# HGRN projections as three passes of rounded operands, with the input split in its norm and the weights split by ScalarE and GpSimd

## The chip, the cores and the metric

The kernel runs on one core of a Trainium2 chip. The metric is the device time of one execution in microseconds.

## The reference, cut to what matters

The program runs three blocks one after another on 512 tokens of width 1024. The change touches the first half of the first block, an HGRN mixer with 16 heads of 128 columns. The part of it that the projections feed:

```python
h  = modulate(x,   norm_g[0], shift,   scale)      # 512 tokens
hc = modulate(ctx, norm_g[0], shift_c, scale_c)    # 256 context tokens
# hgrn_w_in: (1024, 5 * 2048), columns q | v | f forward | f backward | gate
q, v, zf, zb, g = split(h  @ hgrn_w_in)            # q and gate only for the 512 tokens
vc, zfc, zbc    = split(hc @ hgrn_w_in)            # v and both f also for the context
# f = lb + (1 - lb) * sigmoid(z), k = 1 - f; a gated linear recurrence over the tokens,
# forward and backward, started from the context; then an RMS norm per head,
# times silu(g), and a product with hgrn_w_out
```

All inputs and outputs are float32.

## The kernel before, in words

The program is a row of phases. Each phase is one block in which every engine has its own instruction stream, ordered against the others by semaphores that are counted up and waited for; the phases follow one another. `norm_phase` (L382) writes the normed and modulated input to `K.hT` (128 partitions x 8 k-tiles x 512 tokens) and in place to `K.ctxT` (8 x 256). Its ScalarE squares the tiles, TensorE sums them (L417), VectorE takes the reciprocal (L431) and scales each of 8 + 8 tiles (L434), and ScalarE adds the shift with an Identity (L408).

`hgrn_phase` (L438) then works head by head. For head h, TensorE's `project` (L525) makes eight groups of sums over 8 k-tiles, in the order V for the tokens, V for the context, ZF tokens, ZF context, ZB tokens, ZB context, Q, G, which take turns in four PSUM banks (`ps[n % 4]`). In the V groups the input is the stationary operand and the weights, 128 columns wide, are the moving one (L536); there are 4 + 2 tiles of tokens. In the others the weights are stationary and 512 or 256 tokens move (L540). All operands are float32, and the profile shows two records, a weight load and a matmul each, for every float32 product.

The order on TensorE is project(h), then recur(h-1) (L566): the transposes (L574, L576), the scores in small blocks (L550 to L562), the products with kT (L586, L588), the outputs (L592, L597) and a sum for the norm (L601). ScalarE evacuates the groups (L618): a copy for V, Sigmoid for ZF and ZB into `hg_sig`, Silu for Q and G. Between the evacuations it has the logarithms and exponentials of the head before (L632, L638), then the copies of kT (L655). VectorE prepares gates, scans and products (`prepare`, L705) and the states of the recurrence (`recur`, L751). The sigmoids, q and gate have two buffers each, by the parity of the head.

Each of the five weight pieces of a head (128 x 8 x 128, 512 KB) has a buffer of its own, `hg_w0` to `hg_w4`. SP refills it when the last group that reads it has been summed (L503 to L504), and TensorE waits for the transfer itself:

```python
if c == 0:
    pe.wait_ge(w_in[m], 16 * h + 16)
if n >= 4 or not first:
    pe.wait_ge(evac, NG * h + (n - 3))
```

GpSimd only makes masks at the start of this phase (L510 to L521). Other phases, all of `product_phase` (L785), already use three passes of rounded operands: ScalarE rounds the weights to float32r (L865), GpSimd subtracts the rounded from the full ones (L833), and TensorE adds high x high, low x high and high x low in PSUM (L849 to L851), with 512 moving columns in each. `ho`, `m`, `ff`, `mg`, `pb` are tags of such phases.

Of the kernel before, what the change touches and what calls it, by code (L numbers as in the profile page):

```python
# [5 lines left out]
F32 = mybir.dt.float32  # L6
F32R = mybir.dt.float32r
# [430 lines left out]
def hgrn_phase(K, hO):  # L438
# [3 lines left out]
    hT, cT = K.hT, K.ctxT  # L442
# [8 lines left out]
    with ExitStack() as st:  # L451
        W = [K.sb(st, f"hg_w{m}", [P, KD, P]) for m in range(5)]
        vt = [K.sb(st, f"hg_v{i}", [P, NT // P, P]) for i in range(2)]
        sg = [[K.sb(st, f"hg_sig{i}{d}", [P, NT]) for d in range(2)] for i in range(2)]
        qs = [K.sb(st, f"hg_q{i}", [P, T]) for i in range(2)]
        gs = [K.sb(st, f"hg_gate{i}", [P, T]) for i in range(2)]
        f1 = [K.sb(st, f"hg_f{d}", [P, NT]) for d in range(2)]
        kk = [K.sb(st, f"hg_k{d}", [P, NT]) for d in range(2)]
        cum = [K.sb(st, f"hg_cum{d}", [P, NT]) for d in range(2)]
        lev = [K.sb(st, f"hg_lev{d}", [P, 3, T]) for d in range(2)]  # L460
        dg = [K.sb(st, f"hg_diag{d}", [P, 2, T]) for d in range(2)]
# [9 lines left out]
        osq = K.sb(st, "hg_osq", [P, T])  # L471
# [8 lines left out]
        w_in = sems[0:5]  # L480
# [5 lines left out]
        LAST_OF = {V: 2, ZF: 4, ZB: 6, Q: 7, G: 8}  # L486
# [7 lines left out]
        with nc.Block() as block:  # L494
            @block.sync
            def _(sp):
                clear_old(sp, old)

                def load(h, first, shift=0):
                    at = h * P if first else sp.snap(h * P)  # L500
                    for m in (V, ZF, ZB, Q, G):
                        if not first:
                            sp.wait_ge(proj, NG * h + LAST_OF[m])  # L503
                        sp.dma_start(W[m][:, :, :], wv[:, :, bass.ds(at + (COL[m] + shift), P)]).then_inc(w_in[m], 16)  # L504
                load(0, True)
                with sp.Fori(0, NH - 1) as before:
                    load(before, False, P)
# [14 lines left out]

            @block.tensor
            def _(pe):
                def project(h, p, first=False):  # L525
                    for n, (m, c) in enumerate(GROUPS):
                        if c == 0:
# [3 lines left out]
                        src, w = (cT, TC) if c else (hT, T)  # L531
                        bank = ps[n % 4]
                        if m == V:
                            for t in range(w // P):
                                for k in range(KD):
# [30 lines left out]
                def recur(h, p, very_first=False):  # L566
# [34 lines left out]
                    pe.matmul(SC[:, :], K.ones[:, :], osq[:, :], start=True, stop=True).then_inc(ms_ok, 1)  # L601
# [12 lines left out]
            def _(act):  # L614
# [3 lines left out]
                def evacuate(h, p, groups):  # L618
                    for n in groups:
# [6 lines left out]
                        elif m in (ZF, ZB):  # L626
                            s = sg[p][m - ZF]
                            act.activation(ctx_cols(s) if c else lat_cols(s), bank[:, 0:TC if c else T], ACT.Sigmoid).then_inc(evac, 1)
                        else:
                            act.activation((qs if m == Q else gs)[p][:, :], bank[:, :], ACT.Silu).then_inc(evac, 1)  # L630
# [21 lines left out]
                def recur(h):  # L652
# [5 lines left out]
                    act.activation(osq[:, :], OUT[:, :], ACT.Square).then_inc(sq_ok, 1)  # L658
# [1889 lines left out]
```

## Time and profile before

| | us |
|---|---|
| median of 3 runs | 5039.47 (5036.48 to 5039.67) |
| the profiled execution, its time | 5038.89 |
| its span in the profile | 5037.1 |
| hgrn phase, first to last of its matmuls | 271.6 to about 1290 |
| one head in the steady loop | 61.96 |

The granted TensorE clock is 0.87 of full as a mean over the span. In the rows below, "PE" is TensorE's matmuls, "PEld" its weight loads, "DVE" VectorE, "ACT" ScalarE, "POOL" GpSimd. A matmul's duration covers its way through the pipeline, so its price in a stream is read from start to start. Where rows of a timeline say x16, sixteen records in a row are merged, and the time beside it runs from the first one's start to the last one's end.

### The profile page before, as it was taken

The numbers are of one execution on the slowest core, as the hardware profiler recorded it, in microseconds if no ns is written. First come the engines' busy times: TensorE is split into PE (matmuls) and PEld (weight loads), VectorE is DVE, ScalarE is ACT, GpSimd is POOL, SyncE is SP. The second block draws the span as 40 slices with busy tenths as digits, with TensorE's granted clock in tenths as the row PEclk, the third lists the DMA queues.
The fourth block names the chain that finished last, engine by engine and source line by source line (L and its number), as shares of the span: only waits on it lengthen the run. The fifth ranks groups of instructions, "written<-read, shape, count | busy, mean of one in ns | idle before, by whom it ended". The sixth has DMA issues, their size and how long they took to land. (4 is left out here: it accounts for less than half of the span.)

```text
span 5037.1 us, 62135 instructions
## 1 busy us (share of the span) xinstructions
PE 4047.9 (80%) x24211; PEld 2819.7 (56%) x24211; DVE 1802.6 (36%) x3074; ACT 1340.2 (27%) x2208; POOL 697.1 (14%) x366
## 2 busy tenths in 40 slices
PE   6789999999789976865666678898686668687987
PEld 2356666666644433453644566676455547565766
DVE  1034444444249952034033102211227566222222
ACT  0123333333221122222122221322222130323331
POOL 0000000000200001011000133333320010233432
PEclk7799999999899988967656799899798888888998
DMA  8821111110232201110200122222110100222322
GB/s 326 304 63 43 42 42 42 42 42 21 67 96 75 75 21 34 47 36 17 35 1 0 50 63 71 84 83 67 46 52 2 27 25 3 75 72 64 92 77 63
DMA packets 484430, 312.96 MB, mean 62 GB/s; under 512 B 28236, under 2 KB 441477, under 8 KB 484262
## 3 DMA queue, kind: packets, MB, share of 16 engines
q1 hardware_dynamic: 484262, 310.67, 21.0%
q8 instruction: 111, 1.82, 0.2%
q14 instruction: 57, 0.47, 0.0%
HBM read 308.54 MB, written 2.10 MB: 62 GB/s over the span
## 5 line engine op out<-in xcount | busy, mean ns | idle before, releaser
L540 PE MATMUL hg_bank<-hT,hg_w 128*128 128x512 f32 x1024 | 447.3, 592 | 0.0
L997 PE MATMUL cv_bank<-hT,cv_w 128*128 128x512 f32 x768 | 334.1, 596 | 17.0 <-DMA cv_w<-in_conv_w_in_dram 17.0
L1071 DVE SCALAR_TENSOR_TENSOR conv_u<-cv_pad,vec,conv_u 128x512 f32<-128x512 f32 x480 | 318.7, 745 | 0.0
L540 PEld LDWEIGHTS hg_bank<-hT,hg_w 128*128 128x128 f32 x1024 | 193.5, 190 | 223.4 <-issue 221.8
L997 PEld LDWEIGHTS cv_bank<-hT,cv_w 128*128 128x128 f32 x768 | 147.0, 192 | 202.4 <-issue 184.6
L849 PE MATMUL m_bank<-m_rh,m_wh 128*128 128x512 f32 x512 | 204.7, 400 | 65.6 <-POOL m_wl L833 65.6
L850 PE MATMUL m_bank<-m_rl,m_wh 128*128 128x512 f32 x512 | 203.4, 397 | 0.0
L851 PE MATMUL m_bank<-m_rh,m_wl 128*128 128x512 f32 x512 | 203.0, 396 | 0.0
L833 POOL TENSOR_TENSOR m_wl<-m_w,m_wh 128x1024 fp32r<-128x1024 f32 x64 | 152.6, 2387 | 284.5 <-ACT m_wh L865 284.5
L833 POOL TENSOR_TENSOR ho_wl<-ho_w,ho_wh 128x2048 fp32r<-128x2048 f32 x8 | 36.6, 4581 | 1079.5 <-ACT ho_wh L865 1079.5
L849 PE MATMUL mg_bank<-mg_rh,mg_wh 128*128 128x512 f32 x320 | 127.6, 399 | 51.2 <-POOL mg_wl L833 51.2
L849 PE MATMUL ff_bank<-ff_rh,ff_wh 128*128 128x512 f32 x352 | 138.9, 395 | 36.8 <-POOL ff_wl L833 36.8
L754 DVE COPY hg_probe<-hg_bank 128x1 f32<-128x1 f32 x32 | 5.1, 158 | 447.1 <-PE hg_bank L555 447.1
L833 POOL TENSOR_TENSOR mg_wl<-mg_w,mg_wh 128x1024 fp32r<-128x1024 f32 x40 | 94.2, 2379 | 467.5 <-ACT mg_wh L865 467.5
L849 PEld LDWEIGHTS m_bank<-m_rh,m_wh 128*128 128x128 f32 x512 | 98.9, 193 | 88.7 <-issue 68.1
L833 POOL TENSOR_TENSOR z_wl<-z_w,z_wh 128x1024 fp32r<-128x1024 f32 x12 | 28.2, 2373 | 843.7 <-ACT z_wh L865 843.7
L850 PE MATMUL ff_bank<-ff_rl,ff_wh 128*128 128x512 f32 x352 | 137.9, 392 | 0.0
L851 PE MATMUL ff_bank<-ff_rh,ff_wl 128*128 128x512 f32 x352 | 137.9, 392 | 0.0
L536 PE MATMUL hg_bank<-hg_w,hT 128*128 128x128 f32 x1024 | 119.5, 279 | 22.2 <-DMA hg_w<-in_hgrn_w_in_dram 22.2
L536 PEld LDWEIGHTS hg_bank<-hg_w,hT 128*128 128x128 f32 x1024 | 119.3, 195 | 29.8 <-DMA hg_w<-in_hgrn_w_in_dram 22.6
L833 POOL TENSOR_TENSOR ff_wl<-ff_w,ff_wh 128x1024 fp32r<-128x1024 f32 x44 | 103.9, 2383 | 184.3 <-ACT ff_wh L865 184.3
L1587 PE MATMUL at_bank<-ident,at_x 128*128 128x128 f32 x160 | 40.9, 418 | 107.1 <-DVE at_x L1645 107.1
(680 smaller groups left out, 8761.5 us busy)
## 6 DMA issues: line engine op xcount, KB each, us to landing
ada_w<-in_w_ada_dram SPq DMA_DIRECT2D x24, 2048.0 KB, 19.7
hg_w<-in_hgrn_w_in_dram SPq DMA_DIRECT2D x80, 512.0 KB, 3.8
m_w<-in_w_mlp_dram SPq DMA_DIRECT2D x64, 512.0 KB, 4.1
ada_w<-in_ada_w_dram SPq DMA_DIRECT2D x12, 2048.0 KB, 20.0
cv_w<-in_conv_w_in_dram SPq DMA_DIRECT2D x48, 512.0 KB, 3.9
ff_w<-in_w_ffn_in_dram SPq DMA_DIRECT2D x44, 512.0 KB, 5.0
mg_w<-in_w_in_dram SPq DMA_DIRECT2D x40, 512.0 KB, 5.1
fo_w<-in_w_ffn_out_dram SPq DMA_DIRECT2D x16, 704.0 KB, 4.7
```

The costliest lines, as they stand in the source:

```text
L536: ins = pe.matmul(bank[:, t * P:(t + 1) * P], src[:, k, t * P:(t + 1) * P], W[m][:, k, :], start=(k == 0), stop=(k == KD - 1))
L540: ins = pe.matmul(bank[:, 0:w], W[m][:, k, :], src[:, k, 0:w], start=(k == 0), stop=(k == KD - 1))
L754: dve.tensor_copy(probe[:, :], SC[:, 0:1])
L833: ins = pool.tensor_tensor(WL[s % 2][g][:, :, :], W[s % raws][g][:, :, :], WH[s % 2][g][:, :, :].bitcast(F32), ALU.subtract)
L849: pe.matmul(ps[p * 4 + g][:, :], WH[p][g][:, k, :], rh[:, k, :], start=(k == 0), stop=False)
L850: pe.matmul(ps[p * 4 + g][:, :], WH[p][g][:, k, :], rl[:, k, :], start=False, stop=False)
L851: ins = pe.matmul(ps[p * 4 + g][:, :], WL[p][g][:, k, :], rh[:, k, :], start=False, stop=(k == kt - 1))
L997: ins = pe.matmul(ps[n % RING][:, :], W[n % SLOTS][:, k * P:(k + 1) * P], K.hT[:, k, :], start=(k == 0), stop=(k == KD - 1))
L1071: ins = dve.scalar_tensor_tensor(o, x, by, o, ALU.mult, ALU.add)
L1587: pe.transpose(ps[3 + b][:, j * P:(j + 1) * P], X[:, n % 2, b, j * P:(j + 1) * P], K.ident[:, :])
```

## The change

The norm ahead of the phase becomes `split_norm_phase`: VectorE scales a tile into one of four temporary tiles, ScalarE adds the shift and writes the sum rounded to float32r (`hh`, `ch`), and VectorE then computes shifted minus rounded into a second float32r tile (`hl`, `cl`), two tiles later in its order. In `hgrn_phase` the five weight buffers become two, with two rounded (`WH`) and two remainder (`WL`) buffers beside them. A weight piece is a unit u; ScalarE rounds it (`round_unit`) once it has landed and the unit two before has been used by TensorE, and GpSimd subtracts, counting `low`. TensorE waits for `low` in place of the transfer, and SP refills a buffer when `low` says that the piece has been split. Each product becomes three matmuls of float32r operands. The roundings stand in ScalarE's order behind the evacuations of groups 1, 3, 5 (for ZB, Q and G of the same head) and 6 and 7 (for V and ZF of the next). The sigmoids are written straight into `hg_f`, q has one buffer, and gate, `lev`, `dg` and `osq` lie in the tiles `hT` and `ctxT`, which this phase no longer reads.

```diff
+def split_norm_phase(K, jobs):
...
+                for j, (x, hi, lo, w, g, shift, scale, v) in enumerate(jobs):
+                    for k in range(KD):
+                        n = KD * j + k
+                        act.wait_ge(scaled, n + 1)
+                        act.activation(hi[:, k, 0:w], tmp[:, n % 4, 0:w], ACT.Identity,
+                                       bias=K.mod[:, shift + k, v:v + 1]).then_inc(added, 1)
...
+                    for k in range(KD + 2):
+                        if k < KD:
+                            n = KD * j + k
+                            if n >= 4:
+                                dve.wait_ge(low, n - 3)
+                            dve.scalar_tensor_tensor(tmp[:, n % 4, 0:w], x[:, k, 0:w], gain[:, j, k:k + 1], rstd[:, j, 0:w],
+                                                     ALU.mult, ALU.mult).then_inc(scaled, 1)
+                        if k >= 2:
+                            n = KD * j + k - 2
+                            dve.wait_ge(added, n + 1)
+                            dve.scalar_tensor_tensor(lo[:, k - 2, 0:w], tmp[:, n % 4, 0:w], K.mod[:, shift + k - 2, v:v + 1],
+                                                     hi[:, k - 2, 0:w].bitcast(F32), ALU.add, ALU.subtract).then_inc(low, 1)
...
-        W = [K.sb(st, f"hg_w{m}", [P, KD, P]) for m in range(5)]
+        W = [K.sb(st, f"hg_w{m}", [P, KD, P]) for m in range(2)]
+        WH = [K.sb(st, f"hg_wh{m}", [P, KD, P], F32R) for m in range(2)]
+        WL = [K.sb(st, f"hg_wl{m}", [P, KD, P], F32R) for m in range(2)]
...
+                with sp.Fori(1, NH // 2 + 1) as j:
+                    at = sp.snap(j * (2 * P))
+                    for p in range(2):
+                        for n, m in enumerate(ORDER):
+                            u = 5 * p + n
+                            sp.wait_ge(low, 10 * j + (u - 9))
+                            sp.dma_start(W[u % 2][:, :, :], wv[:, :, bass.ds(at + (COL[m] + p * P - 2 * P), P)]).then_inc(w_in[u % 2], 16)
...
+                pool.sem_inc(low, 2)
+                with pool.Fori(0, NH // 2) as j:
+                    for u in range(10):
+                        pool.wait_ge(high, 10 * j + (u + 1))
+                        pool.tensor_tensor(WL[u % 2][:, :, :], W[u % 2][:, :, :], WH[u % 2][:, :, :].bitcast(F32),
+                                           ALU.subtract).then_inc(low, 1)
...
                         if c == 0:
-                            pe.wait_ge(w_in[m], 16 * h + 16)
+                            pe.wait_ge(low, 5 * h + (u + 3))
...
                                 for k in range(KD):
-                                    ins = pe.matmul(bank[:, t * P:(t + 1) * P], src[:, k, t * P:(t + 1) * P], W[m][:, k, :],
-                                                    start=(k == 0), stop=(k == KD - 1))
+                                    pe.matmul(bank[:, a], hi[:, k, a], wh[:, k, :], start=(k == 0), stop=False)
+                                    pe.matmul(bank[:, a], hi[:, k, a], wl[:, k, :], start=False, stop=False)
+                                    ins = pe.matmul(bank[:, a], lo[:, k, a], wh[:, k, :], start=False, stop=(k == KD - 1))
                         else:
                             for k in range(KD):
-                                ins = pe.matmul(bank[:, 0:w], W[m][:, k, :], src[:, k, 0:w],
-                                                start=(k == 0), stop=(k == KD - 1))
+                                pe.matmul(bank[:, 0:w], wh[:, k, :], hi[:, k, 0:w], start=(k == 0), stop=False)
+                                pe.matmul(bank[:, 0:w], wh[:, k, :], lo[:, k, 0:w], start=False, stop=False)
+                                ins = pe.matmul(bank[:, 0:w], wl[:, k, :], hi[:, k, 0:w], start=False, stop=(k == KD - 1))
...
+                def round_unit(j, p, u):
+
+                    n, h = (p + u) % 2, 2 * j + p
+                    act.wait_ge(w_in[n], 80 * j + 16 * ((5 * p + u) // 2 + 1))
+                    if u >= 2:
+                        act.wait_ge(proj, NG * h + (LAST[u - 2] + 1))
+                    elif not isinstance(j, int) or h > 0:
+                        act.wait_ge(proj, NG * h + (LAST[u + 3] + 1 - NG))
+                    act.activation(WH[n][:, :, :], W[n][:, :, :], ACT.Copy).then_inc(high, 1)
...
+                            s = f1[m - ZF]
+                            if not first:
+                                act.wait_ge(k_ok, 2 * h + (m - ZF - 1))
...
+                        elif m == Q:
+                            if not first:
+                                act.wait_ge(prod_ok, 2 * h)
+                            act.activation(qs[:, :], bank[:, :], ACT.Silu).then_inc(evac, 1)
...
+                        if n in (1, 3, 5):
+                            round_unit(j, p, 2 + n // 2)
+                        elif n >= 6 and not last:
+                            round_unit(j + p, 1 - p, n - 6)
```

## Rows read from the trace of the kernel before

**Rows 1.** The page: the engines, and its costliest group.

```profile
PE 4047.9 (80%) x24211; PEld 2819.7 (56%) x24211; DVE 1802.6 (36%) x3074; ACT 1340.2 (27%) x2208; POOL 697.1 (14%) x366
...
L540 PE MATMUL hg_bank<-hT,hg_w 128*128 128x512 f32 x1024 | 447.3, 592 | 0.0
```

**Rows 2.** Windows: length, busy time and instructions of each engine, clock, DMA share.

```profile
364.00:1230.00 866.00, 856.40 (x5822) 593.49 (x5821) 385.17 (x756) 321.17 (x602) 0.00 (x0) 1.00 0.14 40
...
691.03:752.99 61.96, 61.27 (x418) 42.44 (x416) 27.51 (x54) 22.94 (x44) 0.00 (x0) 1.00 0.14 42
...
3299.89:3303.97 4.08, 4.08 (x19) 3.38 (x18) 0.00 (x0) 0.17 (x1) 2.39 (x1) 1.00 0.13 37
```

**Rows 3.** Tile hg_bank: a wait of TensorE, us in total and times.

```profile
  DVE hg_ks L749: 41.5, 2
```

**Rows 4.** Timeline of TensorE, one head: start us, length us, instruction.

```profile
691.03 7.31 PE L536 MATMUL hg_bank<-hg_w,hT 128*128 128x128 f32 x64
698.18 3.74 PE L536 MATMUL hg_bank<-hg_w,ctxT 128*128 128x128 f32 x32
701.75 7.03 PE L540 MATMUL hg_bank<-hT,hg_w 128*128 128x512 f32 x16
708.62 3.62 PE L540 MATMUL hg_bank<-ctxT,hg_w 128*128 128x256 f32 x16
712.08 7.03 PE L540 MATMUL hg_bank<-hT,hg_w 128*128 128x512 f32 x16
...
736.13 0.49 PE L574 MATMUL hg_bank<-ident,hg_ks 128*128 128x128 f32 x3
```

**Rows 5.** Timeline of TensorE in the m phase, 18 matmuls apart.

```profile
3299.89 0.39 PE L851 MATMUL m_bank<-m_rh,m_wl 128*128 128x512 f32 x1
...
3303.97 0.39 PE L851 MATMUL m_bank<-m_rh,m_wl 128*128 128x512 f32 x1
```

**Rows 6.** Timeline row and source row of L292: 4 moving columns.

```profile
62.00 1.05 PE L292 MATMUL ada_bank<-ada_pick,ada_sums 128*128 128x4 f32 x8
...
L292 PE MATMUL ada_bank<-ada_pick,ada_sums x288: 252/253/376, 44.9 to 233.3; 128*128 128x4 f32 x144
```

**Rows 7.** Weight loads of rounded and of f32 operands: ns min/median/max.

```profile
L849 PEld LDWEIGHTS m_bank<-m_rh,m_wh x512: 187/188/335, 3186.8 to 3590.4; 128*128 128x128 f32 x171
...
L536 PEld LDWEIGHTS hg_bank<-hg_w,hT x1024: 186/192/334, 271.6 to 1193.6; 128*128 128x128 f32 x171
```

**Rows 8.** Timeline of the norm's end and the first projection.

```profile
254.12 5.39 DVE L434 SCALAR_TENSOR_TENSOR hT<-xT,norm_gain,norm_rstd 128x512 f32<-128x512 f32 x8
...
261.21 3.26 DVE L434 SCALAR_TENSOR_TENSOR ctxT<-ctxT,norm_gain,norm_rstd 128x256 f32<-128x256 f32 x8
...
271.59 3.78 PE L536 MATMUL hg_bank<-hg_w,hT 128*128 128x128 f32 x16 [22.21 <-DMA hg_w<-in_hgrn_w_in_dram]
```

**Rows 9.** Rounding and subtraction in other phases: ns min/median/max.

```profile
L833 POOL TENSOR_TENSOR m_wl<-m_w,m_wh x64: 2342/2389/2398, 3184.3 to 3581.8; 128x1024 fp32r<-128x1024 f32 x64
...
L833 POOL TENSOR_TENSOR pb_wl<-pb_w,pb_wh x14: 2345/2951/2953, 3645.7 to 3717.5; 128x1024 fp32r<-128x1024 f32 x14
...
L865 ACT ACTIVATE m_wh<-m_w x64: 1052/1056/1064, 3183.2 to 3580.7; 128x1024 fp32r<-128x1024 f32 x64
```

**Rows 10.** Timeline of ScalarE in the same head.

```profile
722.60 0.38 ACT L628 ACTIVATE hg_sig<-hg_bank 128x256 f32<-128x256 f32 x1 [2.86 <-PE hg_bank L540]
723.00 1.28 ACT L630 ACT_TABLE_LOAD   x1
...
737.26 0.38 ACT L656 ACTIVATE hg_kT<-hg_bank 128x256 f32<-128x256 f32 x1
```

**Rows 11.** The page's DMA issues: KB each, median us to landing.

```profile
hg_w<-in_hgrn_w_in_dram SPq DMA_DIRECT2D x80, 512.0 KB, 3.8
```

**Rows 12.** Timeline of VectorE in the same head.

```profile
715.22 0.95 DVE L749 TENSOR_TENSOR hg_ks<-hg_ks,hg_k 128x768 f32<-128x768 f32 x1
740.33 0.16 DVE L754 COPY hg_probe<-hg_bank 128x1 f32<-128x1 f32 x1 [24.16 <-PE hg_bank L555]
```

More of the change, by code:

```diff
@@ L479, in hgrn_phase @@
         sems, old = K.phase()
-        w_in = sems[0:5]
+        w_in = sems[0:2]
+        high, low, used = sems[2:5]
         (proj, evac, set0, lb_ok, f_ok, g_ok, k_ok, cum_ok, dif_ok, rd_ok, exp_ok, prod_ok, tr_ok, trc_ok, sc_ok,
@@ L485, in hgrn_phase @@
         NG = len(GROUPS)
-        LAST_OF = {V: 2, ZF: 4, ZB: 6, Q: 7, G: 8}
+        ORDER = (V, ZF, ZB, Q, G)
+        LAST = (1, 3, 5, 6, 7)
         def ctx_cols(t):
@@ L600, in recur @@
                     pe.wait_ge(sq_ok, h + 1)
-                    pe.matmul(SC[:, :], K.ones[:, :], osq[:, :], start=True, stop=True).then_inc(ms_ok, 1)
+                    pe.matmul(SC[:, :], K.ones[:, :], osq, start=True, stop=True).then_inc(ms_ok, 1)
                 project(0, 0, True)
@@ L616, in _, with evacuate @@
                 act.activation(tmp2[:, :], tmp[:, :], ACT.Exp).then_inc(g_ok, 1)
-                def evacuate(h, p, groups):
+                def round_unit(j, p, u):
[6 more added lines that the diff above has]
+                    act.activation(WH[n][:, :, :], W[n][:, :, :], ACT.Copy).then_inc(high, 1)
+                def evacuate(j, p, groups, first=False, last=False):
+                    h = 2 * j + p
                     for n in groups:
@@ L663, in recur, with step @@
                     act.activation(ors[:, :], ors[:, :], ACT.Exp, scale=-0.5).then_inc(rs_ok, 1)
-                def step(h, p):
+                def step(j, p, last=False):
+                    h = 2 * j + p
                     logs(h - 1)
                     exps(h - 1, 0)
-                    evacuate(h, p, range(0, 2))
+                    evacuate(j, p, range(0, 2))
                     exps(h - 1, 1)
-                    evacuate(h, p, range(2, NG))
+                    evacuate(j, p, range(2, NG), last=last)
                     recur(h - 1)
-                evacuate(0, 0, range(NG))
-                step(1, 1)
-                with act.Fori(1, NH // 2) as j:
-                    step(2 * j, 0)
-                    step(2 * j + 1, 1)
+                round_unit(0, 0, 0)
+                round_unit(0, 0, 1)
+                evacuate(0, 0, range(NG), first=True)
+                step(0, 1)
+                with act.Fori(1, NH // 2 - 1) as j:
+                    step(j, 0)
+                    step(j, 1)
+                step(NH // 2 - 1, 0)
+                step(NH // 2 - 1, 1, True)
                 logs(NH - 1)
@@ L1099, in first_block @@
     inp = K.inp
-    norm_phase(K, [(K.xT, K.hT, T, K.at["norm_g"], 0, 8, 0), (K.ctxT, K.ctxT, TC, K.at["norm_g"], 0, 8, 1)])
     with ExitStack() as st:
         hO = K.sb(st, "hgrn_out", [P, NH, T])
-        hgrn_phase(K, hO)
+        with ExitStack() as s2:
+            hh, hl = (K.sb(s2, f"hg_x_{n}", [P, KD, T], F32R) for n in ("high", "low"))
+            ch, cl = (K.sb(s2, f"hg_ctx_{n}", [P, KD, TC], F32R) for n in ("high", "low"))
+            split_norm_phase(K, [(K.xT, hh, hl, T, K.at["norm_g"], 0, 8, 0), (K.ctxT, ch, cl, TC, K.at["norm_g"], 0, 8, 1)])
+            hgrn_phase(K, hO, hh, hl, ch, cl)
         on_act, on_dve = residual(K, 16, 0)
```

87 lines of the change are left out of this document (61 added, 26 removed).

## The prediction

> **What bounds the kernel now.** I read the page first for where the time is, then the stretch of the hgrn phase alone, then one head of it in order of time. The page says that TensorE is busy for 80% of the span and that an f32 projection line of this phase is its costliest group [rows 1]. That is an average over many phases, so the question is what ends a head. Over the 866 us in which the loop runs steadily, TensorE is busy for 856.40 at full granted clock; VectorE has 385 and ScalarE 321, GpSimd nothing [rows 2]. The waits of the phase's PSUM tile agree: TensorE waited for VectorE's products twice only, 41.5 us together [rows 3], outside this stretch. So a head costs what its TensorE instructions cost: 61.96 us from one head's V group to the next one's, 691.03 to 752.99 [rows 2].
>
> Inside that head [rows 4]: V takes 691.03 to 701.75, **10.72** us for 96 records (48 f32 products of 128 columns, two records each: **0.1117** a record). A group of 512 columns takes 701.75 to 708.62, **6.87** us for 16 records; ZF, ZB, Q and G have one each. A context group of 256 columns takes 708.62 to 712.08, **3.46** us; ZF and ZB have one each. From 736.13 to the end of the window at 752.99, 16.86 us, is the recurrence, which the change leaves alone.
>
> **The change, part by part.**
>
> *The 512-column groups.* Each f32 product becomes three rounded ones. The trace has exactly this form in another phase: from 3299.89 to 3303.97 there are 18 of them, **0.2267** each, each with its own weight load, at full clock [rows 5, 2]. 24 make 5.44 us against 6.87: −1.43, four times a head **−5.72**.
>
> *The V groups.* Here the weights are the moving operand and are only 128 columns wide, with the input as the stationary one. 48 products become 144 instructions of 128 columns, each with a weight load of 128 columns. No row shows a rounded matmul narrower than 512. From below: a quarter of 0.2267, 0.057, if only columns count. Against it stands the weight load. The f32 line L292 moves 4 columns past 128 loaded ones, and eight of its records take 1.05 us with the last one's 0.25 in it: (1.05−0.25)/7 = 0.114 each, with nearly no columns to move [rows 6]. A rounded operand's load lasts as long as an f32 one's, 188 against 192 ns [rows 7]. So 0.1117 to 0.114 is what a load costs when nothing covers it. On top, the rounded matmul of 512 columns takes 0.2267 where f32 needs 0.2163 (3.46/16) for a record of 256 columns, which streams the array as long: some 0.010 more [rows 4, 5]. I take **0.120** for a narrow one, between 0.1117 and 0.125 (0.114 + 0.011). V: 144 × 0.120 = 17.28 against 10.72, **+6.56**. From above: a narrow rounded product might get nothing from its format and cost as a whole f32 product of its width, 2 × 0.1117 = 0.223; that is the second case below. I choose the load's price, because the f32 records of the same shape, 0.1117, and L292's lie there [rows 4, 6].
>
> A page speaks for less. The Trainium skill, "TensorE: Matmul & The Clock Gate", section "Back-to-back issue gap", gives a sustained 81 ns for matmuls of 128 columns with their loads; estimated by it, V is 11.7 us and the change wins (the third case). The same section gives 131 ns for 512 columns, where this trace has 227 [rows 5], so I trust the trace.
>
> *The context groups.* 24 rounded ones of 256 columns each: half of 0.2267 is 0.113, the load's price the same; with the 0.010 again 0.120, so 2.88 against 3.46: −0.58, twice **−1.16**.
>
> *Sum per head:* −5.72 −1.16 +6.56 = −0.32; 16 heads, **−5.1** us.
>
> *The split norm.* VectorE is the longer engine there: eight scalings take 5.39 us together and eight 3.26 [rows 8]. As many subtractions of the same form and widths enter its queue, two tiles behind: 5.39 + 3.26 = **+8.7** us, in the open, since TensorE has nothing until hgrn. The waits for ScalarE's Identity are behind the next scaling and cost nothing; without that cover, some 0.2 each.
>
> *The first weights.* TensorE now starts when the transfer lands, 271.59 [rows 8]. After it come a rounding (1.06) and GpSimd's subtraction (2.39) [rows 9]: **+3.6** with the hand-overs. At the end of the phase nothing is added: no projection stands between the last recurrences, and TensorE waits for products there as before (about half of the 41.5 [rows 3]).
>
> *Rounding and subtracting in the loop.* Five a head: 5.3 us on ScalarE (busy 22.94 of 61.96 [rows 2]) and 12 on GpSimd, idle so far. Costed at nothing; the cover is the group between. The tightest is G: its buffer comes free when ZB has ended, and Q alone, 5.44 us, covers the sigmoid of 0.38, the rounding 1.06 and the subtraction 2.39, together 3.9 with hand-overs; a Silu table load of 1.28 ahead of it would make it 5.2; and in another phase the subtraction took 2.95 [rows 9, 10]. Behind G's evacuation the next ZF is rounded ahead of the copies of kT; these ended at 737.64 and TensorE uses them behind the scores, which VectorE saw done at 740.33, so 1.06 fits [rows 10, 12]. Q's rounding stands behind the exponentials of d=1, and has all of ZB to be ready in.
>
> *The transfers.* SP has the same five 512 KB pieces a head, now waiting for GpSimd's `low` through two buffers. A piece lands in 3.8 us [rows 11]; the nearest need is a group (5.4 us) and a half later. Nothing.
>
> *Single buffers.* Sigmoids go straight into `hg_f`, Q's Silu waits for the products of the head before: these ended at 716.2, Q's Silu comes behind the table load at 723.00 and its own sums, and moves later if at all [rows 10, 12]. Nothing.
>
> **Sum:** −5.1 + 8.7 + 3.6 = +7.2 on the profiled execution's 5038.89 (span 5037.1), 5046.1; the median of the runs is 0.6 above that execution: **5047**. By the ends of the narrow price (0.1117 with 0.1134 for 256 columns; 0.125 for both): per head −1.84 or +0.64, so 5022 to 5062. About 0.2%, 10 us, is what a measurement of this kernel can tell from no change.
>
> **The rivals.**
>
> *Second, the narrow matmul is slow:* a rounded V product costs 0.223, like f32. For it: the trace has no rounded matmul under 512 columns, each is 0.010 dearer than its columns, and nothing proves that the saving of the format does not depend on width. Against: the loads alone explain all narrow rows seen. V 144 × 0.2234 = 32.2, +21.5; −5.72 −1.16 gives +14.6, 16 heads +233, with 12.3 for norm and start +245: **5285**, slower. Then the change would not do in V what its name says: three passes where f32 costs one product. If the 256-column groups go that way too (24 × 0.433 = 10.4 each, +13.9 a head in place of −1.16): near 5525.
>
> *Third, faster:* the weight load of a rounded operand hides fully, and a narrow one costs its columns, 0.057. V 8.2 (−2.56), context 2.72 (−0.74 twice): −9.8 a head, −156 + 12.3: **4895**. The whole change turns to a gain where a V matmul costs less than 0.117: (10.72 + 5.72 + 1.16 − 12.3/16)/144. The page's 81 ns lies between, by estimate near 4952. Against: equal load durations [rows 7]. The page's section "Weight-path perf modes" gives fast loads to inputs other than FP32; whether a rounded operand counts, no row but that shows.
>
> *Fourth, late weights:* TensorE waits in front of G. It needs the chain to pass 5.44: sigmoid, table load, rounding and the slow subtraction together, 5.7 plus hand-overs, 0.5 to 1 us a head, +8 to +16: about **5060**. GpSimd is said to share its SBUF interface with VectorE (Trainium skill, "GPSIMD Engine Reference", section "Specifications"); the 2.95 beside 2.39 [rows 9] fits it, but in Q's time VectorE stands idle until 740.33 [rows 12].
>
> **How the numbers follow.** The forecast 0.46, second 0.37 (its wide form 0.03 more), third 0.08, fourth 0.06. The first and second are far apart because one price, 144 × 16 instructions, is not in the trace. Range: from the low end of the first to the second with a wider narrow price (0.2268, 5293): 5020 to 5296, which leaves out the third and the wide form. The likeliest case's own range is 5022 to 5062. Within 0.2% falls 0.20, from the first case; faster: third 0.08 and the low end of the first 0.05, 0.13; slower 0.67.
>
> **What would show it.** The start-to-start time of the V matmuls: 0.112 to 0.125 forecast, 0.21 to 0.23 second, under 0.1 third. V's stretch 16 to 18, 30 to 33, or 8 to 12 us a head. The 512-column groups at 5.44 and the context ones near 2.9. GpSimd's subtraction named as releaser of a G matmul would show the fourth. The first projection matmul some 12 us later. If the 512-column groups are not at 0.227, or TensorE is no longer busy nearly all of the loop, the whole sum is wrong.

## The result, and the profile after the change

| | before | after |
|---|---|---|
| median of 4 runs each, side by side | 5039.39 us | 5156.9 us (5149.84 to 5159.85) |
| ratio | | **1.0232**, 95% interval 1.0217 to 1.0247 |
| profiled execution, its span | 5038.89, 5037.1 us | 5155.74, 5154.0 us |

The change makes the kernel 117.5 us slower by the medians; the two profiled executions, by which the account below goes, are 116.9 apart. The forecast was 5047; the time lies inside the range of 5020 to 5296, in the gap between its first two cases.

The page of the kernel after: its span, the share of each engine, the instruction queue of section 3 (packets, MB, share of 16 engines), and the costliest lines of the phase (busy us, mean ns, idle before).

```profile
span 5154.0 us, 65691 instructions
...
q8 instruction: 174, 2.85, 0.2%
...
L597 POOL TENSOR_TENSOR hg_wl<-hg_w,hg_wh 128x1024 fp32r<-128x1024 f32 x80 | 223.7, 2796 | 843.2 <-ACT hg_wh L708 843.2
...
L616 PE MATMUL hg_bank<-hg_wh,hg_x_high 128*128 128x128 f32 x512 | 174.9, 342 | 50.8 <-POOL hg_wl L597 34.0
L621 PE MATMUL hg_bank<-hg_x_high,hg_wh 128*128 128x512 f32 x512 | 205.7, 402 | 0.0
```

The instruction queue moved 174 packets; on the page of the kernel before that line reads:

```profile
q8 instruction: 111, 1.82, 0.2%
```

It looks like a footnote, with 0.2% of the DMA engines' time, and I had not looked at it. The stretches of the phase after, with the columns of [rows 2] (length, busy PE, PEld, DVE, ACT, POOL with counts, granted clock, DMA share, GB/s):

```profile
364.00:1230.00 866.00, 840.23 (x6494) 751.88 (x6492) 347.46 (x675) 350.50 (x599) 180.19 (x64) 0.90 0.14 41
806.91:837.69 30.78, 30.78 (x145) 30.78 (x145) 17.56 (x31) 6.95 (x15) 0.00 (x0) 0.50 0.00 1
883.27:899.70 16.43, 16.43 (x146) 16.19 (x145) 14.13 (x24) 9.99 (x18) 0.00 (x0) 1.00 0.00 1
837.69:844.68 6.99, 6.99 (x25) 5.62 (x26) 1.02 (x4) 5.67 (x13) 2.39 (x1) 0.78 0.23 66
899.70:905.17 5.47, 5.47 (x26) 4.55 (x26) 4.41 (x10) 5.24 (x13) 3.86 (x1) 1.00 0.01 3
521.88:526.12 4.24, 1.12 (x2) 0.29 (x3) 1.45 (x3) 3.84 (x4) 0.00 (x0) 1.00 0.01 4
401.37:461.92 60.55, 59.86 (x514) 53.30 (x513) 28.16 (x54) 27.80 (x49) 15.73 (x5) 1.00 0.16 45
806.91:946.89 139.98, 136.08 (x1025) 122.23 (x1025) 55.67 (x109) 55.59 (x97) 27.71 (x10) 0.88 0.13 39
281.37:312.15 30.78, 30.78 (x145) 30.78 (x145) 0.00 (x0) 0.60 (x1) 2.27 (x1) 0.50 0.12 35
```

In the steady stretch the granted clock is 0.90 where [rows 2] have 1.00: that alone says that not one price but a state of the clock has changed. The next rows are two V stretches of neighbouring heads, the same 144 instructions: **30.78 us at a granted clock of 0.50, which is 1.2 GHz, and 16.43 at 1.00, 2.4 GHz**. A head with the fast V takes 60.55 us (401.37 to 461.92), 1.41 less than the 61.96 of before: what the forecast said a head would do, a little better. A pair with one slow V takes 139.98.

Which V is slow, TensorE in order of time tells. First the end of a head that is followed by a slow one, then the end of a head that is followed by a fast one (start, us, engine, line, operation, and in brackets the idle time before it and what ended it).

```profile
803.14 1.13 PE L683 MATMUL hg_bank<-hT,ones 128*128 128x512 f32 x2 [0.69 <-ACT hT L761]
806.91 0.47 PE L616 MATMUL hg_bank<-hg_wh,hg_x_high 128*128 128x128 f32 x1 [2.65 <-issue]
807.18 0.41 PE L617 MATMUL hg_bank<-hg_wl,hg_x_high 128*128 128x128 f32 x1
807.39 0.41 PE L618 MATMUL hg_bank<-hg_wh,hg_x_low 128*128 128x128 f32 x1
...
1302.75 1.12 PE L683 MATMUL hg_bank<-hT,ones 128*128 128x512 f32 x2 [0.69 <-ACT hT L761]
1303.31 0.62 PE L616 MATMUL hg_bank<-hg_wh,hg_x_high 128*128 128x128 f32 x1
1303.77 0.28 PE L617 MATMUL hg_bank<-hg_wl,hg_x_high 128*128 128x128 f32 x1
1303.88 0.28 PE L618 MATMUL hg_bank<-hg_wh,hg_x_low 128*128 128x128 f32 x1
```

From the start of the sum of squares (L683) to V it is 0.56 us in a fast head and 3.65 to 4.24 in a slow one, and the idle time in it is put down to "issue": nothing that the profile shows held it back. The clock falls late in this gap or just behind it: from 521.88 to 526.12, the longest step, it is still 1.00, and the V that follows has 0.6 us at full clock and takes 30.23 us; the others at 1.2 GHz take 30.77 to 30.78. The waits of TensorE in the phase count them (line, what it waited for, us in total, times, longest):

```profile
PE hg_bank L616 <- POOL hg_wl L597: 34.0, 1, 34.0
PE hg_bank L656 <- DVE hg_ks L857: 20.3, 1, 20.3
PE hg_bank L616 <- issue: 16.8, 6, 3.1
PE hg_bank L683 <- ACT hT L761: 11.0, 16, 0.7
```

Six times: at 526.12, 666.76, 806.91, 946.89, 1087.05 and 1227.15, every second head. TensorE's loop has two heads in its body and seven turns, so six backward jumps, and V of the even head stands right behind each. A head behind a jump costs 19.1 us more than a warm one: a pair is 140.2 on the mean of the five, where two warm heads are 121.1. Of that 3.1 to 3.7 is the longer step to V, 14.35 is V (30.78 − 16.43), and 1.5 is the next group of 512 columns, 6.99 at a mean clock of 0.78 against 5.47 [837.69 and 899.70 above].

**Where the 117 us are.** 15 heads times −1.41 is −21; six jumps times 19.1 are +115. The first head, whose V too runs at 1.2 GHz from its first to its last instruction (30.78; before, the first head's V took 9.76 + 3.57 = 13.33), takes 59.84 us from its V to the second's (281.37 to 341.21) where it took 47.71 (271.59 to 319.30), +12. With +9.8 for the later start (281.37 against 271.59) that makes +115, and the executions differ by 116.9.

**The theory: the jump (A in the expectations).** The loop's body on TensorE has grown from 192 to 288 projection instructions a head, and the sequencer now fetches it anew at each turn; the idle gap that follows lets the clock fall, and a stream of narrow rounded matmuls does not bring it back up. It has two forms: the length of the body brings the gap (A1), or something else in the loop's turn does (A2). The rivals: the rounded narrow matmul has two prices of its own, with alternate buffers, whatever stands ahead of it; or the gap is a wait for GpSimd's or ScalarE's semaphores that the profile misnames. The Trainium skill has a rule that fits A, in "Runtime: NRT & Kernel Launch", section "Instruction fetch mechanics": "Branching breaks sequential prefetch", a taken branch whose target is not in the sequencer's window has to fetch it before it goes on. The packets of the instruction queue fit it, 174 against 111.

### The profile page after: what moved, and what is told of

Read it like the earlier page. It is cut to its first block and busy times, and to the rows that moved or that the text cites. A ratio compares the mean times of both kernels' runs of the same rounds, so it can differ in the third digit from the quotient of the medians.

```text
span 5154.0 us, 65691 instructions
## 1 busy us (share of the span) xinstructions
PE 4136.1 (80%) x25747; PEld 3094.8 (60%) x25747; DVE 1817.5 (35%) x3090; ACT 1419.7 (28%) x2288; POOL 921.3 (18%) x446
## 5 line engine op out<-in xcount | busy, mean ns | idle before, releaser
L597 POOL TENSOR_TENSOR hg_wl<-hg_w,hg_wh 128x1024 fp32r<-128x1024 f32 x80 | 223.7, 2796 | 843.2 <-ACT hg_wh L708 843.2
L616 PE MATMUL hg_bank<-hg_wh,hg_x_high 128*128 128x128 f32 x512 | 174.9, 342 | 50.8 <-POOL hg_wl L597 34.0
L621 PE MATMUL hg_bank<-hg_x_high,hg_wh 128*128 128x512 f32 x512 | 205.7, 402 | 0.0
L622 PE MATMUL hg_bank<-hg_x_low,hg_wh 128*128 128x512 f32 x512 | 203.5, 397 | 0.0
L623 PE MATMUL hg_bank<-hg_x_high,hg_wl 128*128 128x512 f32 x512 | 203.0, 396 | 0.0
L618 PE MATMUL hg_bank<-hg_wh,hg_x_low 128*128 128x128 f32 x512 | 171.9, 336 | 0.0
L617 PE MATMUL hg_bank<-hg_wl,hg_x_high 128*128 128x128 f32 x512 | 171.8, 336 | 0.0
L616 PEld LDWEIGHTS hg_bank<-hg_wh,hg_x_high 128*128 128x128 f32 x512 | 129.3, 253 | 58.1 <-POOL hg_wl L597 34.4
```

The lines of the kernel that those rows point to most:

```text
L597: pool.tensor_tensor(WL[u % 2][:, :, :], W[u % 2][:, :, :], WH[u % 2][:, :, :].bitcast(F32), ALU.subtract).then_inc(low, 1)
L616: pe.matmul(bank[:, a], hi[:, k, a], wh[:, k, :], start=(k == 0), stop=False)
L618: ins = pe.matmul(bank[:, a], lo[:, k, a], wh[:, k, :], start=False, stop=(k == KD - 1))
L621: pe.matmul(bank[:, 0:w], wh[:, k, :], hi[:, k, 0:w], start=(k == 0), stop=False)
L622: pe.matmul(bank[:, 0:w], wh[:, k, :], lo[:, k, 0:w], start=False, stop=False)
L623: ins = pe.matmul(bank[:, 0:w], wl[:, k, :], hi[:, k, 0:w], start=False, stop=(k == KD - 1))
```

## The experiments

Each kernel ran beside the kernel before on the same chip. E1 to E4 went together (before: 5033.79), then E5 to E8 (before: 5043.60), then E9 and E10 (before: 5037.37).

### E1: the loop on TensorE written out

```diff
-                with pe.Fori(1, NH // 2) as j:
+                for j in range(1, NH // 2):
```

> The changed kernel with TensorE's loop over pairs of heads written out, so that its stream has no backward jump; same matmuls, same waits. Theory A (the jump back leaves TensorE idle for 3.7 us, the clock falls to 1.2 GHz, and the narrow rounded matmuls do not raise it): the six heads behind a jump become like the others, each 19.1 us shorter, V at 16.4 us in place of 30.8, no wait of TensorE ahead of V; about 5042 us. Rival B (the wait ahead of V is one for weights or for ScalarE, and comes every second head whatever the code's form): no change, 5157. Rival C (narrow rounded matmuls fall to the low clock by themselves): V stays at 30.8 in some heads although no gap is ahead of it.

Measured: 5035.62 (10 runs), ratio 1.0006, interval 0.9996 to 1.0015. Nothing else was changed, neither an instruction's work nor a wait. No gap is left, and every V but the first head's takes 16.42 to 16.43:

```profile
364.00:1230.00 866.00, 856.40 (x7273) 762.36 (x7272) 399.72 (x766) 396.41 (x682) 225.93 (x72) 1.00 0.15 44
886.74:903.16 16.42, 16.42 (x146) 16.18 (x145) 14.12 (x24) 9.99 (x18) 0.00 (x0) 1.00 0.01 2
```

All of the loss but some 2 us hangs on the jump. (The instruction queue moved 163 packets here too: more code in a straight line costs nothing that the waits show; it is the jump back that does.) The rivals are out: the same buffers, semaphores and waits stand there, and no V behind the first is slow.

### E2: the loop cut at another place

The body now begins behind V of the even head; V's two groups stand at its end.

```diff
-                with pe.Fori(1, NH // 2) as j:
-                    project(2 * j, 0)
+                project(2, 0, part=range(0, 2))
+                with pe.Fori(1, NH // 2 - 1) as j:
+                    project(2 * j, 0, part=range(2, 8))
                     recur(2 * j - 1, 1)
                     project(2 * j + 1, 1)
                     recur(2 * j, 0)
+                    project(2 * j + 2, 0, part=range(0, 2))
...
```

> The changed kernel with TensorE's loop cut at another place: the jump back now lies between the V groups and the ZF group of an even head, all else the same. Theory A: V no longer starts behind a gap and stays at 16.4 us; the fetch falls behind queued V matmuls or costs up to 4 us ahead of 512-wide matmuls, which run at the high clock or regain it soon; 5042 to 5066 us. Rival B (a wait for weights): the gap stays ahead of V, 5157. Rival C: V slow without a gap.

Measured: 5047.09 (10 runs), ratio 1.0027 (1.0017 to 1.0037). This lies in the expected range. The gaps have moved with the jump, ahead of ZF's group of 512 columns (L623 here), and there are five, as there are five jumps:

```profile
PE hg_bank L623 <- issue: 8.6, 5, 2.0
```

They are shorter, 1.5 to 2.0 us, and V stays at 16.43 in all heads but the first. The group of 512 columns behind the gap takes 7.19, 7.20 and 6.89 us in three of the five heads and 5.57 and 5.56 in the other two, where the granted clock stayed at 1.00. So this shorter gap in front of wide matmuls costs itself and at most 1.7 us; the one in front of narrow rounded ones costs itself and some 16.

### E3: wide matmuls between the gap and V

Twelve extra rounded matmuls of 512 columns in the loop ahead of V of each even head; V overwrites what they leave.

```diff
+                        if n == 0:
+                            for i in range(lift):
+                                pe.matmul(bank[:, :], wh[:, i % KD, :], hi[:, i % KD, :], start=True, stop=True)
...
-                    project(2 * j, 0)
+                    project(2 * j, 0, lift=12)
```

> The changed kernel with 12 more rounded matmuls of 512 columns between the jump and the V groups of each even head of the loop (results overwritten). Theory A: the gap of 3.7 us stays; the 12 run first at 0.43 and then at 0.23 us, some 4 us together, and lift the clock, so V takes 16.4 in place of 30.8; per such head -14.4 -1.5 +4: about -12, six or seven heads, 5075 to 5095 us. A rival that explains the slow V by something other than the clock that the gap left (contention for SBUF, late remainders, a loop's first V): V stays at 30.8 and the time rises by 7 times 4 to 5, to about 5187.

Measured: 5084.18 (4 runs), ratio 1.0097 (1.0079 to 1.0114), 73 us less than the changed kernel though it does more. The twelve, then V:

```profile
528.39:533.52 5.13, 5.13 (x12) 4.02 (x13) 5.10 (x9) 1.76 (x2) 0.00 (x0) 0.52 0.02 3
533.52:549.55 16.03, 16.03 (x145) 16.03 (x144) 12.20 (x23) 5.06 (x12) 0.00 (x0) 1.00 0.00 1
```

The gap of 2.5 to 2.9 us is still there, six times. The twelve run at a granted clock of 0.52, and V behind them at 1.00 in 16.03 us. (In the six heads behind a jump the twelve take 4.2 to 5.3 us; where it is 5.3, the clock is back only within V's first 0.7 us.) So gap and low clock are two links of the chain, and the second can be cut alone: the clock comes back behind twelve wide matmuls, and behind 144 narrow ones it does not.

### E4: a shorter body, by leaving out one pass

The pass of the high weights with the low input is left out of all groups but V: 240 projection instructions a head in place of 288.

```diff
-                                pe.matmul(bank[:, 0:w], wh[:, k, :], lo[:, k, 0:w], start=False, stop=False)
```

> The changed kernel without the high-weights times low-input pass in all groups but V: this part of the computation is left out, V is as it was, the loop and its jump as well, and the loop's code is 96 matmuls of about 800 shorter. Theory A1 (the gap is the fetch of a loop body that is too long to stay in the sequencer's memory): the gap goes, V at 16.4 in all heads behind the first; -115 for that and -16 x (32 x 0.228 + 16 x 0.12 = 9.2) = -147: about 4895 us. Rival A2 (any jump back costs the gap with rounded matmuls, whatever the length): only the second part, V still 30.8 in six heads, about 5010 us.

Measured: 5033.72 (10 runs), ratio 0.9994 (0.9984 to 1.0004). Both numbers are missed, 4895 by far and 5010 by 24 us. The jump still costs what it did, the instruction queue moved 173 packets, and TensorE has a new wait of about 1 us, for GpSimd's subtraction ahead of ZB and of Q, most often in the heads that stand behind no jump:

```profile
PE hg_bank L621 <- POOL hg_wl L597: 20.8, 23, 1.7
...
PE hg_bank L616 <- issue: 16.7, 6, 3.0
```

With jumps as before and that wait on top, 5010 + 20.8 is 5031, near what was measured. Either the body was not short enough, or its length is not what matters. This run alone leaves A open, so two more looked at it from both sides.

### E5: a body as long as before's

Two passes everywhere: V without the high input with the low weights, the others without the high weights with the low input. That is 192 instructions a head, as many as before has records.

```diff
-                                    pe.matmul(bank[:, a], hi[:, k, a], wl[:, k, :], start=False, stop=False)
...
-                                pe.matmul(bank[:, 0:w], wh[:, k, :], lo[:, k, 0:w], start=False, stop=False)
```

> The changed kernel with two passes in every group: low input is left out of the groups with stationary weights, low weights out of V. So many parts of the computation are missing; what is looked at is the jump. The loop body has 2 x 192 projection matmuls in place of 2 x 288, as many weight loads and matmuls as the kernel before. Theory A1 (a body over some length is fetched anew at each jump): no wait ahead of V, V at 96 x 0.115 = 11.0 in all heads but the first, some 60 instruction packets fewer. Rival A2 (the gap belongs to any jump of this kernel): 3 to 4 us ahead of V in six heads and V near 20 there.

Measured: 4932.57 (one run). The page's instruction queue, and the waits of TensorE:

```profile
q8 instruction: 111, 1.82, 0.2%
...
PE hg_bank L620 <- POOL hg_wl L597: 98.4, 31, 6.4
PE hg_bank L616 <- POOL hg_wl L597: 34.0, 1, 34.0
```

No wait is put down to issue; the loop and all its jumps are still there. The instruction queue is back at 111 packets, to the packet what the kernel before has. V behind a jump takes as long as any other, 7.5 + 3.57 us for its 96 products. So it is the length that decides, between 192 and 240 projection instructions a head. With groups this short, TensorE waits for GpSimd ahead of ZB instead, 6.3 us a head, and it could be asked whether these waits only hide the gap; E9 has the same short body without them.

### E6: V as f32 products of the high operands

V takes the high input and the high weights alone, read as f32, without the remainders: 48 products, 96 records.

```diff
-                                    pe.matmul(bank[:, a], hi[:, k, a], wh[:, k, :], start=(k == 0), stop=False)
-                                    pe.matmul(bank[:, a], hi[:, k, a], wl[:, k, :], start=False, stop=False)
-                                    ins = pe.matmul(bank[:, a], lo[:, k, a], wh[:, k, :], start=False, stop=(k == KD - 1))
+                                    ins = pe.matmul(bank[:, a], hi[:, k, a].bitcast(F32), wh[:, k, :].bitcast(F32), start=(k == 0), stop=(k == KD - 1))
```

> The changed kernel with V as f32 products of the rounded operands read as float32 (the remainders are left out of V): the same width of 128, 48 products in place of 144 rounded matmuls. Theory A with a part that it adds (a stream of f32 records raises the clock, one of narrow rounded matmuls with a load each doesn't): if a gap is left ahead of V, V starts slow and is at full clock after some microseconds, 13 to 14 us in place of 30.8. Rival (any V behind a gap stays slow to its end): 10.72 x 2 = 21.4 us.

Measured: 5018.29 (one run). The gap stays (173 packets), and in nine heads TensorE now waits for GpSimd's subtraction too, 30.6 us in all. V behind the gap, and the first of it in order of time:

```profile
502.81:515.17 12.36, 12.36 (x96) 12.36 (x97) 12.29 (x20) 6.43 (x15) 0.00 (x0) 0.86 0.01 3
```

```profile
502.81 9.03 PE L616 MATMUL hg_bank<-hg_wh,hg_x_high 128*128 128x128 f32 x64 [2.73 <-issue]
```

12.36 us at a mean clock of 0.86, against 7.14 + 3.49 in a warm head: the f32 stream of the same shapes works its way back to 2.4 GHz within some microseconds, the rounded one does not in 30. The kernel before shows the same in its first head, whose V, also behind a long wait, cost only 2.6 us more than a warm one (9.76 against 7.14).

### E7: the kernel before with a longer body

Nothing is rounded here; the loop on TensorE has four heads in its body, and two backward jumps.

```diff
-                with pe.Fori(1, NH // 2) as j:
-                    project(2 * j, 0)
-                    recur(2 * j - 1, 1)
-                    project(2 * j + 1, 1)
-                    recur(2 * j, 0)
+                for h in (2, 3):
+                    project(h, h % 2)
+                    recur(h - 1, 1 - h % 2)
+                with pe.Fori(1, NH // 4) as j:
+                    for q in range(4):
+                        project(4 * j + q, q % 2)
+                        recur(4 * j + (q - 1), 1 - q % 2)
```

> The kernel before, with TensorE's loop body made of four heads (three passes, two backward jumps), nothing else. Theory A1: at the two jumps a gap of 3 to 5 us ahead of V, which the kernel before has nowhere, then V at 10.7 to 14, since it is f32; about +10 to +15 us in all. Rival A2: no gap, the time of before.

Measured: 5051.83 (one run, above all seven runs of before beside it, 5039.35 to 5046.73). Its instruction queue and its wait:

```profile
q8 instruction: 154, 2.52, 0.2%
...
PE hg_bank L536 <- issue: 5.1, 2, 2.6
```

Two jumps, two gaps, in a kernel that has no rounded projection at all. The gap belongs to a long body and not to the change's arithmetic. Behind it V's first four tiles take 9.83 and 8.87 us in place of 7.14, so here a jump costs 4.4 to 5.4 us, not 19.

### E8: V with its weights stationary

If both the jump and the narrow stream are to go, V can be computed as the other groups are: the weights loaded, 512 or 256 columns of input moving. That is 24 + 24 instructions in place of 144, and gives V transposed, so six transposes a head at the start of the recurrence turn it back, with ScalarE's copies behind them; ScalarE's evacuation of V, with the rounding of ZB's weights that follows it, moves ahead of the exponentials of d=0. All three passes are kept.

```diff
-                        if m == V:
-                            for t in range(w // P):
...
+                        if d == 0:
+                            if not very_first:
+                                pe.wait_ge(o1_ok, h)
+                            for n in range(4):
+                                pe.transpose(OUT[:, n * P:(n + 1) * P], vT[p][:, (2 + n) * P:(3 + n) * P], K.ident[:, :])
+                            for n in range(2):
+                                pe.transpose(KV[:, (2 + n) * P:(3 + n) * P], vT[p][:, n * P:(n + 1) * P], K.ident[:, :])
...
```

> The changed kernel with V computed like the other groups: weights stationary, 512 or 256 inputs moving, and six transposes a head behind it at the start of the recurrence, with two more copies on ScalarE; V is evacuated ahead of the exponentials of d=0. Theory A (both losses of the change lie in narrow rounded matmuls, their price of a load each and the low clock they cannot leave, and in the gap of the long body): V 24 x 0.228 + 24 x 0.12 = 8.35 in place of 16.4, transposes +0.7, no long body, no slow heads; 5157 - 115 - 16 x 7.4 + some stalls for weights of 0 to 2 us a head: 4925 to 4960 us, faster than both kernels. Rival D (with V so short the rounding and subtraction end last): a wait for GpSimd of 3 us or more in every head, 4990 or more.

Measured: 5017.80 (4 runs), ratio 0.9947 (0.9930 to 0.9964). No gap, 111 packets, V at 5.85 + 2.87 us; but 60 to 90 us of the expected gain are missing, as rival D of the expectation has it. TensorE waits, and the start of Q in one of these heads and GpSimd's row before it say for what:

```profile
PE hg_bank L614 <- POOL hg_wl L598: 100.3, 16, 34.5
```

```profile
652.11 0.79 PE L614 MATMUL hg_bank<-hg_x_high,hg_wh 128*128 128x512 f32 x1 [4.48 <-POOL hg_wl L598]
```

```profile
648.14 6.17 POOL L598 TENSOR_TENSOR hg_wl<-hg_w,hg_wh 128x1024 fp32r<-128x1024 f32 x2 [13.20 <-ACT hg_wh L708]
```

```profile
647.00 1.06 ACT L708 ACTIVATE hg_wh<-hg_w 128x1024 fp32r<-128x1024 f32 x1
647.95 0.87 ACT L722 ACTIVATE hg_f<-hg_bank 128x512 f32<-128x512 f32 x2
648.69 1.08 ACT L708 ACTIVATE hg_wh<-hg_w 128x1024 fp32r<-128x1024 f32 x1
```

With V so short, the projections run ahead of ScalarE, whose roundings of Q's and G's weights stand behind the exponentials of both directions, Q's behind ZF's sigmoids as well and G's behind ZB's (L722). Q's comes at 647.00 and G's at 648.69. GpSimd subtracts the two in a row, Q's in 3.84 us from 648.14 to 651.98, and Q waits some 4.5 us a head. The waits also lower the clock in part: from 652.11 to 665.30, the two groups Q and G, it is 0.82, and they take 13.2 us where 10.9 is their time at full clock.

### E9: the same, with one rounding moved forward

```diff
-                        if n in (1, 3, 5):
+                        if n in (1, 5) or (n == 3 and first):
...
                     exps(h - 1, 0)
+                    round_unit(j, p, 3)
                     exps(h - 1, 1)
```

> The kernel with the wide V, with the rounding of Q's weights moved on ScalarE from behind the evacuation of the ZF context to between the exponentials of d=0 and of d=1. In the run before it TensorE waited 4.5 us a head for Q's remainder, and ran the next group partly at 1.2 GHz (12.4 to 13.7 us for Q and G in place of 10.9). If that rounding was only late in ScalarE's order: the wait goes, 4.5 + about 2 us a head, 16 x 6.5 = 104: about 4915 us. If GpSimd's subtraction (up to 5 us beside VectorE's products) is what ends last: a wait of 1 to 3 us stays, 4950 to 4990 us.

Measured: **4917.09** (5 runs, 4914.73 to 4930.25), ratio **0.9769** (0.9753 to 0.9786): 2.3% under the kernel before and 4.7% under the changed one, with the whole computation. Only the first wait for weights is left, and a head takes 53.57 us. Nothing is put down to issue, with six jumps and 112 packets on the instruction queue, and no other wait stands there that could hide a gap. It is a close fit: from 604.95 to 611.53 GpSimd takes 6.58 us for Q's remainder, and Q starts at 611.67.

```profile
PE hg_bank L614 <- POOL hg_wl L598: 34.0, 1, 34.0
```

```profile
371.94:425.51 53.57, 52.88 (x425) 45.32 (x423) 34.11 (x54) 28.33 (x51) 16.37 (x5) 1.00 0.17 50
```

### E10: E1, with the clock raised ahead of the very first V

E1's loop written out, and E3's twelve matmuls once, ahead of the first head.

```diff
-                project(0, 0, True)
+                project(0, 0, True, lift=12)
```

> The changed kernel with TensorE's loop written out and 12 more rounded matmuls of 512 columns ahead of the very first V group only. If the low clock is what makes the first head's V take 30.8 us: 16 to 16.4 there, the 12 themselves about 4.5 to 5, so -10 against the written-out kernel: about 5026 us. If the first head is slow for its cold buffers or first transfers: V stays at 30.8 and the time is 5 us longer, 5041.

Measured: 5023.41 (5 runs), ratio 0.9970 (0.9957 to 0.9984). The five runs lie between 5019.63 and 5039.89, and the profiled one is the longest. The twelve take 4.43 us, and the first V behind them 10.67 + 5.36 us where it took 30.78. Of it:

```profile
288.00:305.00 17.00, 17.00 (x143) 16.57 (x143) 0.00 (x0) 2.75 (x4) 0.76 (x1) 1.00 0.00 1
```

So the changed arithmetic, as written and with the full clock in every V, beats the kernel before by 0.3%.

## Why the prediction was right or wrong

**Right: the prices at full clock.** A narrow rounded matmul was put at 0.120, between 0.1117 and 0.125; it is 11.07 / 96 = 0.1153 in V's four tiles and 5.36 / 48 = 0.1117 in the context's two. A group of 512 columns was put at 5.44 and is 5.47; a context group was put at 2.88 and is 2.87. The sum per head was −0.32 and is −1.41: of the difference 0.85 is V, 17.28 against 16.43, and 0.40 is a term that I did not have, the step from the sum of squares to V, 0.56 against 0.96. The argument from the weight load [rows 6, 7] fits what came, though no run takes the load apart from the matmul. The 81 ns of the Trainium skill ("TensorE: Matmul & The Clock Gate", section "Back-to-back issue gap"), and with them the third case, did not come.

**Right: norm and start.** From the first scaling to the last subtraction it is 18.8 us (252.11 to 270.92) where it was 10.35 [rows 8], +8.5 against +8.7; from there to the first projection 10.45 against 7.12, +3.3 against +3.6. The 9.8 seen in the absolute start is these 11.8 less 2.0 that this execution was early already before the norm.

**Right: the cover in the loop.** No wait for weights stands in the changed kernel behind its first; the fourth case did not come. But it was nearer than I said: I gave the subtraction 2.95 us at most, from another phase, and here it takes up to 5.10. The instructions of the tile, then three of them in order of time:

```profile
L597 POOL TENSOR_TENSOR hg_wl<-hg_w,hg_wh x80: 2346/2396/5101, 279.0 to 1338.1; 128x1024 fp32r<-128x1024 f32 x80
```

```profile
419.41 5.05 POOL L597 TENSOR_TENSOR hg_wl<-hg_w,hg_wh 128x1024 fp32r<-128x1024 f32 x1 [30.33 <-ACT hg_wh L708]
427.82 3.54 POOL L597 TENSOR_TENSOR hg_wl<-hg_w,hg_wh 128x1024 fp32r<-128x1024 f32 x1 [3.36 <-ACT hg_wh L708]
436.16 2.40 POOL L597 TENSOR_TENSOR hg_wl<-hg_w,hg_wh 128x1024 fp32r<-128x1024 f32 x1 [4.80 <-ACT hg_wh L708]
```

The slow ones are ZB's and Q's, beside VectorE's products. ZB's ends at 424.46, and the group that needs it starts at 426.21, 1.75 us later. G's, which the forecast called the tightest, takes 2.40 and ends at 438.56, 1.46 us before its group at 440.02. With shorter groups these subtractions became TensorE's wait: ahead of ZB and Q in E4, of ZB in E5, of Q in E8.

**Wrong: a step that is not in the sum.** "The change part by part" prices the projection's instructions, 192 records a head turned into 288, and says of the recurrence behind them that the change leaves it alone. It never asks what 96 more instructions a head do to the loop that holds them. That is where the 117 us are: the body no longer stays with the sequencer (174 packets against 111; E5 and E7 turn this off and on by length alone), each of six jumps idles TensorE for 2.5 to 3.1 us, and V behind it runs at 1.2 GHz. With the jumps gone and the full clock in every V (E10) the kernel is 14 us faster than before, inside the −17 to +23 that the likeliest case spanned.

**Wrong: a clock taken for granted.** The sum has one price for each instruction, read at a granted clock of 1.00 [rows 2]. The same instruction costs 0.2133 at 1.2 GHz (10.24 / 48, the context's V), and whether V is at one or the other depends on what stands ahead of it: a gap of 2.5 to 3.1 us, or twelve wide matmuls behind that gap (E3). The first head could have warned me: it stands behind the long wait for weights, where nobody had to jump, and I had [rows 2] for the steady stretch only. It accounts for 12 of the 117.

**The rivals.** The second one came near the time by another way. It put V at 32.2 us in all 16 heads, since the format would save nothing at that width; V is 30.2 to 30.8 in seven heads and 16.43 or less in nine, and E1 shows the width to be innocent. That the range held the time is owed to that case's wrong mechanism, and should not be taken for a forecast of this one. No case named the jump.

**Open.** At what length between 192 and 240 projection instructions a head the gap begins. That the gap is a fetch of the body is inferred from its length and the packets and was not seen itself; packets alone make no gap (163 in E1). Why a stream of narrow rounded matmuls, with TensorE busy throughout, stays at 1.2 GHz where f32 records of the same shape come back. V in f32 with its own unrounded operands, beside rounded groups, was not tried, as the phase has no room for both copies of the input.

## What to carry to other kernels

Whoever turns one instruction into three inside a loop should count the loop's body on that engine, not only the work: read the instruction queue's packets and look for "issue" ahead of the first instruction behind the jump. Never let a jump or a long wait be followed by narrow rounded matmuls; put wide ones there, or write the product so that it is wide in the first place, which here took V from 16.43 to 8.72 us, for 0.65 us of transposes, and with one rounding moved turned +2.3% into −2.3%. When TensorE gets faster, look at once for what its weights wait for: moving one ScalarE instruction ahead was worth some 90 us between E8 and E9 (by their ratios, 0.9947 and 0.9769).

## What the runs showed of the hardware that I had not expected

- A backward jump on TensorE leaves no idle time put down to issue as long as the body is short (before, E5, E8, E9: 192 projection records a head, two heads), and 2.5 to 3.1 us where it is long (after, E3, E4, E6, E7; 1.5 to 2.0 where wide matmuls stand behind it, E2). The Trainium skill, "Runtime: NRT & Kernel Launch", section "Instruction fetch mechanics", speaks of a DMA fetch of the target's page; the packets fit it (111 or 112 without a gap, 154 to 174 with one), but no run shows the fetch itself.
- After a gap of 2.5 to 3.1 us the granted clock is 0.50; behind E2's gaps of 1.5 to 2.0 it fell in three of five. Behind twelve rounded matmuls of 512 columns, which take 4.2 to 5.3 us, it is back at 1.00 (E3, E10), with f32 records of 128 columns in less than 9 us (E6); with 144 rounded matmuls of 128 columns it did not come back in 30.8 us, in any of seven heads.
- GpSimd's subtraction of 128x1024 takes 2.39 us by itself and up to 5.10, in E9 up to 6.59, beside VectorE's products. The Trainium skill, "GPSIMD Engine Reference", section "Specifications", says that the two share an SBUF interface; the rows fit that, with a factor of two and more, though no run took VectorE's products away.
